# Sampled attention of a hybrid decoder layer: how far the gathers of keys and values run ahead of the one they wait for

## The reference, cut to what matters

```python
s_c = jnp.einsum('bqgnd,bgcd->bgnqc', qblk, kc) * scale - sl * dist_c     # compressed blocks
p_c, _ = masked_softmax(s_c, dist_c >= 0)
imp = jnp.einsum('bgnqc,cj->bgqj', p_c, overlap)
score = jnp.where(j_idx <= jt, imp + FORCE_BONUS * forced, -jnp.inf)
top, idx = lax.top_k(score, topn)                                         # 16 of 65 blocks
kv_sel = gather_fn(idx)                                                   # rows through the page table
s_s = jnp.einsum('bqgnd,bgqkld->bgnqkl', qblk, kv_sel[:, :, :, :, 0]) * scale - slopes * dist_s
p_s, _ = masked_softmax(s_s.reshape(B, G, n, qb, topn * SLC_LEN), mask)
o_s = jnp.einsum('bgnqm,bgqmd->bqgnd', p_s.astype(v_sel.dtype), v_sel)
o_a = gb[..., 0:1] * o_cmp + gb[..., 1:2] * o_slc + gb[..., 2:3] * o_win
```

## Time and profile before

| | before |
|---|---|
| median of 3 runs | 1964.57 us (1963.92 to 1968.91) |
| the profiled execution | 1965.92 us, of which its span is 1964.1 us |
| PE busy | 1739.6 us, 89% of the span |
| DVE busy | 1100.1 us, 56% |
| POOL busy | 425.0 us, 22% |
| DMA queue q0 (issued by GpSimd) | 131.93 MB, 20.5% of 16 engines |
| DMA queue q1 (issued by SP) | 176.72 MB, 29.4% of 16 engines |

### The profile page before, as it was taken

The page is one execution under the profiler, slowest core; times in us unless marked ns, Lnnn a source line. Parts: engine busy times, 40 slices in busy tenths (PEclk is TensorE's granted clock), DMA queues, the critical chain, the costliest instruction groups (busy, mean ns, idle before and its releaser), DMA issues. The chain is left out here.

```text
span 1964.1 us, 38854 instructions
## 1 busy us (share of the span) xinstructions
PE 1739.6 (89%) x16171; PEld 1513.6 (77%) x16171; DVE 1100.1 (56%) x1937; ACT 565.4 (29%) x1216; POOL 425.0 (22%) x525
## 2 busy tenths in 40 slices
PE   4999888998989985899998898677699999999998
PEld 1898777887988985899986455554597999999776
DVE  3114666667665333699884455365387544444456
ACT  1224433322212211243433475323363300000000
POOL 0000900000001302332311589634200000000500
PEclk7999999988999987899997899889899999999999
DMA  6546674353545755666753633387675133323232
GB/s 234 152 118 199 172 244 136 116 160 104 157 138 170 234 189 192 214 208 187 228 142 143 258 98 87 117 276 245 213 233 155 66 91 93 87 86 131 88 98 76
DMA packets 241285, 311.14 MB, mean 158 GB/s; under 512 B 41557, under 2 KB 192493, under 8 KB 235222
## 3 DMA queue, kind: packets, MB, share of 16 engines
q1 hardware_dynamic: 211862, 176.72, 29.4%
q0 software_dynamic: 29248, 131.93, 20.5%
HBM read 281.19 MB, written 79.61 MB: 184 GB/s over the span
## 5 line engine op out<-in xcount | busy, mean ns | idle before, releaser
L302 PE MATMUL inp_acc<-hh,inp_wh 128*128 128x272 f32 (+1 forms) x1072 | 343.2, 320 | 33.4 <-DVE inp_wl L274 18.5
L302 PE MATMUL inp_acc<-hh,inp_wl 128*128 128x272 f32 (+1 forms) x1072 | 317.1, 296 | 0.0
L302 PE MATMUL inp_acc<-hl,inp_wh 128*128 128x272 f32 (+1 forms) x1072 | 316.5, 295 | 0.0
L302 PEld LDWEIGHTS inp_acc<-hh,inp_wh 128*128 128x128 f32 (+1 forms) x1072 | 208.4, 194 | 55.6 <-issue 28.9
L274 DVE TENSOR_TENSOR inp_wl<-inp_w,inp_wh 128x1024 fp32r<-128x1024 f32 (+1 forms) x67 | 81.2, 1212 | 247.7 <-ACT inp_wh L454 247.3
L302 PEld LDWEIGHTS inp_acc<-hl,inp_wh 128*128 128x128 f32 (+1 forms) x1072 | 209.1, 195 | 3.5 <-issue 3.3
L302 PEld LDWEIGHTS inp_acc<-hh,inp_wl 128*128 128x128 f32 (+1 forms) x1072 | 208.1, 194 | 0.4
L564 POOL DMA_DIRECT2D out_dram<-in_cache_dil_dram x84 | 42.9, 514 | 531.6 <-PE inp_acc L302 512.1
L1411 PE MATMUL cmp_pH<-cmp_RTh,cmp_w1h 128*128 128x256 f32 (+1 forms) x512 | 148.8, 291 | 0.0
L269 DVE CAST trk_wh<-trk_w 128x1024 fp32r<-128x1024 f32 x62 | 46.7, 754 | 179.5 <-PE trk_pz L283 124.2
L1411 PE MATMUL cmp_pH<-cmp_RTl,cmp_w1h 128*128 128x256 f32 (+1 forms) x512 | 145.9, 285 | 0.0
(11 more groups left out here) (597 smaller groups left out, 3823.7 us busy)
## 6 DMA issues: line engine op xcount, KB each, us to landing
inp_w<-in_w_in_dram SPq DMA_DIRECT2D x66, 512.0 KB, 5.9
trk_w<-in_w_ffn_dram SPq DMA_DIRECT2D x66, 512.0 KB, 3.9
out_dram<-in_cache_dil_dram POOLq DMA_DIRECT2D x64, 511.0 KB, 5.6
sdi_kv<-in_cache_dil_dram SPq DMA_DIRECT2D x288, 64.0 KB
ringA<-in_w_ada_dram SPq DMA_DIRECT2D x16, 1024.0 KB, 7.3
PT<-inp_o SPq DMA_DIRECT2D x58, 272.0 KB, 4.0
ada_wada<-in_w_ada_dram SPq DMA_DIRECT2D x8, 1024.0 KB, 17.6
out_dram<-in_cache_dil_dram POOLq DMA_DIRECT2D x16, 508.0 KB, 8.2
```

What stands on the lines that cost most here:

```text
L302: i = pe.matmul(out, l, r, start=(first and n == 0), stop=(last and n == 2))
```

## The change

A piece is issued when the piece three places ahead of it has landed, in place of two places. So up to three pieces (six indirect DMAs) are under way at a time, in place of two (four). Pieces 4, 5 and 6 now start without such a wait; piece 7 waits for piece 4. The other waits, the ring and all instructions of all engines are as before, and stand in the same order.

```diff
-            if i >= 6:
-                pool.wait_ge(self.got[(i - 2) % self.R], self.arrived(self.pieces[i - 2]))
+            if i >= 7:
+                pool.wait_ge(self.got[(i - 3) % self.R], self.arrived(self.pieces[i - 3]))
             for g in range(GRP):
                 pool.indirect_dma_start(out=self.slot((x, b, h))[:, g * 1024:(g + 1) * 1024], out_offset=None, in_=src,
```

## The result

The changed kernel is **slower**: 1996.33 us median of 4 runs (1991.83 to 1999.02), the kernel before beside it 1966.74 (1963.92 to 1974.35, 4 runs). The ratio is 1.0127, 95% interval 1.0101 to 1.0153: 25 us, where the forecast had a gain of 14.7. The profiled execution took 1999.02 us with a span of 1997.2, 33.1 more than the span of before. Nearly all of it lies in the phase of the change: the trunk's first matmul starts at 1447.68, and in the kernel before at 1414.6. Three of the four runs of before had been made for the prediction; the fourth, 1974.35 us, came with the changed kernel's, and against it alone the loss is 1.1%.

A forecast was written before the change was run, and what follows sets the result against it. TensorE, busy for 89% of the span, was taken to wait for gathered pieces in three places. Gains of 1.0 + 6.2 + 7.5 = 14.7 us gave 1950 us; a range of 1944 to 1960 held somewhat over 8 in 10.

The forecast's parts named there:

- The rate, the landings and GpSimd's path: In the tail, GpSimd resumes every 2.7 to 3.0 us and q0 moves over 330 GB/s.
- So the wait for a landing is the one that moves: GpSimd's issue of pieces: places are free in time, so waiting for landings is what the third piece shortens.
- The predicted signs on TensorE: Waits at u = 12 gone, S(10) to S(12) 10 to 11 us, V(12) 29 to 31 us after piece 27's issue.
- First stretch: Up to piece 7, beside SP's stores: a deeper q0 fills gaps where it was short of work, gaining 1.0 us.
- Middle and tail: Middle: both waits for pieces at u = 12 vanish, 6.2 us; tail: pieces 27 to 35 land closer together, 7.5 us.
- slower: Rival, 1971 us, chance 0.04: pieces are served side by side, so a third takes its share from those ahead.

The follow-up runs named there:

- e8: Third piece under way only for pieces ahead of place 15, two from there on; against the kernel before, ratio 0.9994.
- e15: Plain transfers from fixed rows in place of gathers from place 15 on, two pieces under way; against the kernel before, ratio 0.9963.
- e11: Plain transfers from fixed rows in place of gathers from place 15 on, three pieces under way there, two before; against the kernel before, ratio 0.9926.
- e13: Changed kernel with a pause of six small memsets on GpSimd ahead of every third piece; against the kernel before, ratio 0.9949.
- e17: Changed kernel with a pause of four small memsets on GpSimd ahead of every second piece; against the kernel before, ratio 0.9970.
- e7: Changed kernel with gathered rows of 1 KB, not 4 KB, from place 15 on, two pieces under way before it; against the kernel before, ratio 1.0120.

## Why the prediction was wrong

*The rate, the landings and GpSimd's path*: right. Pieces go out 2.5 us apart, q0 moves 376 to 389 GB/s where over 330 was said, and TensorE's waits for pieces are down from 21.1 us to the 1.5 us that stand ahead of V(4) in both traces.

**The step that failed** is "So the wait for a landing is the one that moves", with the sentence ahead of it, that compression had more than six gathers in flight "without a longer issue". I looked there at GpSimd's issues and at q0, and not at what TensorE did beside them. Twelve back-to-back gathers cost TensorE nothing in the trace of before, but the trace of after, whose code is the same there, has this row of waits for PE in 784:812:

```profile
PE cmp_pH L1411 <- issue: 5.1, 6, 1.8
```

This row, of 3.6 to 5.3 us, stands in nine of the seventeen traces: in that of after and in all of chips 4 and 6. So the price that the prediction put at nothing was there, and the one trace that it was read from didn't show it. With the third piece GpSimd gathers 103 rows per us for as long as places are free (from 1394.28 to 1414.88, 20 us), TensorE is held up, and as the places come free only by TensorE's steps, GpSimd waits for those in turn and then starts the next run. The predicted signs on TensorE failed accordingly: V(12) was to come 29 to 31 us after the issue of piece 27, and piece 35 was only issued 32 us after it; the phase is 32 us longer. In the kernels with the third piece in the middle, in the tail and in the first stretch alone, the middle costs 21 us, the tail 6 and the first nothing that can be told, where 6.2, 7.5 and 1.0 us of gain were forecast.

*First stretch*: 1.0 us was forecast, with 0 by the rule of the Trainium skill (DMA: Bandwidth & Descriptors, Queues, rings and completion order). e8 gives 0.9994 (0.9974 to 1.0015), which can't tell 1 us from none, and doesn't contradict the rule.

*Middle and tail*: 6.2 + 7.5 us were forecast. With TensorE nearly free, e15 and e11 show 7 us (1 to 13) for the third piece, with plain transfers, and e13 10 us (5 to 15) against before, with gathers and pauses. So the terms may be too large, but no run shows it. From the issue of piece 27 to that of piece 35's second half it takes 31.4 us before, 25.2 in e15 and 20.7 in e11: part of the time between landings goes already when GpSimd's transfers are the shorter ones, with two under way.

*The rivals*: "slower" was on record at 0.04, for service side by side. It was to decide only while pieces stay more than some 3.5 us apart; at 389 GB/s one takes 1.049 / 0.389 = 2.7 us, and TensorE hardly waits for pieces any more, so that mechanism isn't what happened. No rival had TensorE itself slowed, and the range ended 36 us below the time.

## What to carry to other kernels

A deeper queue of gathers also changes what GpSimd does: it issues gathers for 10 or 20 us on end, and on some chips TensorE pays. Before deepening one, look in several executions, and on several chips, for idle time put down to "issue" beside the runs of gathers that are already there, above all with no semaphore to explain it, and for late starts of the engines that read TensorE's results. Where it appears, a short rest for GpSimd ahead of each piece (0.7 to 1.4 us here) took the loss away, and the largest gain measured with it was 0.23%. On chips where it doesn't appear, the deeper queue with pauses gave 0.3 to 0.5%. And run the unchanged change beside each remedy on the same chip: here e11 to e17 can't tell the remedy from the chip, because that run is missing.

## What was not expected of the hardware

- In the traces of after and of chips 4 and 6, GpSimd's gathers of 128 rows, one every 1.24 us, go with TensorE's instructions coming only one or two per 0.7 us, and with a semaphore that VectorE waits for coming 12 us late. It is the same at 106 GB/s (e7) as at 389. VectorE's and ScalarE's own instructions keep their durations.
- In the traces of chips 0 and 12 the same twelve gathers in compression cost TensorE nothing, in seven of seven.
- On chip 0, plain transfers at 405 GB/s on the same queue cost TensorE nothing; on chips 0 and 12, gathers of 64 and 96 rows at the same intervals hardly anything (0.5 and 0.7 us of "issue"). A gather takes GpSimd 0.89, 0.91 and 0.94 us for 64, 96 and 128 rows, so fewer rows hardly make it quicker.
- A stall begins some 3 to 7 us into a run (1317.2 after 1313.77; 1401.4 after 1394.28; in e7 1398.6 after 1393.28) and ends 2 to 3 us after its last gather (1417.11 after 1414.88; in e7 1415.78 after 1412.98).

Open: what GpSimd's gathers share with TensorE; why chips 4 and 6 show the stalls and chips 0 and 12 don't; how the changed kernel itself does on chips 0 and 12; whether the rows per us decide, or the length of a run; and whether the recording of the execution, which is on in every trace, plays a part.
